# Idle products of TensorE removed at five places of a hybrid decoder layer

## The reference

```python
mix = hybrid_mixer(x, ...)                       # ends in: merged @ w_out
x = layer_norm(ALPHA * x + mix, ln1_g, ln1_b)
aff = sigmoid(x2 @ router_w); sel = aff + router_bias
# best group of experts by its two best sel; the two best experts in it
gate = w_sel / sum(w_sel)
# tokens are sorted by expert into blocks of 128
h = silu(xblk @ w_gate[e]) * (xblk @ w_up[e]);  y = h @ w_down[e]
x = layer_norm(ALPHA * x + sum of the token's two gate * y, ln2_g, ln2_b)
```

## Time and profile before

| | us |
|---|---|
| median of three runs | 2181.05 |
| the profiled execution | 2181.75 |
| its span | 2179.9 |
| attention, 705 to 860 | 155 |
| output projection's last part and choice, 1500 to 1526 | 26 |
| routing, 1526 to 1540 | 14 |
| experts, 1540 to 2129 | 589 |
| joining, 2129 to the end | 51 |

### The profile page before, as it was taken

One profiled execution on the slowest core, in us unless ns is written; L12 is line 12 of the kernel. 1 busy time (PEld: TensorE's weight loads), 2 busy tenths in 40 slices (PEclk: granted clock), 3 DMA queues, 4 the chain that ended last, 5 costly groups with the idle time before them and its releaser, 6 DMA issues. The chain is left out here.

```text
span 2179.9 us, 36484 instructions
## 1 busy us (share of the span) xinstructions
PE 2088.2 (96%) x14738; PEld 1681.1 (77%) x14739; DVE 1267.1 (58%) x1270; ACT 928.4 (43%) x1067; POOL 504.1 (23%) x357
## 2 busy tenths in 40 slices
PE   8999999999999999999999999998799999999996
PEld 6777777766787787888887788787588888888882
DVE  4767322224411465346478713455788888888885
ACT  4662122233101464022245421001577777777763
POOL 3332211113250001333423332200122222222200
PEclk9999999999999999999999999999799999999998
DMA  4445634434430543321143422121799999999986
GB/s 153 134 118 188 182 101 117 113 96 157 171 135 24 137 110 125 137 68 48 48 131 115 168 90 97 61 78 58 295 406 389 383 383 382 382 376 382 380 336 236
DMA packets 138136, 408.48 MB, mean 187 GB/s; under 512 B 38736, under 2 KB 60112, under 8 KB 112800
## 3 DMA queue, kind: packets, MB, share of 16 engines
q1 hardware_dynamic: 122528, 363.21, 48.3%
q10 hardware_dynamic: 6128, 26.22, 3.1%
q0 software_dynamic: 9360, 17.32, 2.1%
HBM read 353.53 MB, written 69.93 MB: 194 GB/s over the span
## 5 line engine op out<-in xcount | busy, mean ns | idle before, releaser
L3458 DVE TENSOR_TENSOR ex_sb_low<-landed,high 128x2048 fp32r<-128x2048 f32 x192 | 431.1, 2287 | 66.1 <-ACT high L3387 63.8
L3387 ACT CAST high<-landed 128x2048 fp32r<-128x2048 f32 x186 | 345.9, 1910 | 40.2 <-PE ex_ps_u L166 37.3
L3272 POOL DMA_INDIRECT y_rows<-ex_sb_y,slot_row x32 | 32.2, 1007 | 443.3 <-ACT ex_sb_y L3402 425.1
L164 PE MATMUL ex_ps_g<-high,ex_sb_xt 128*128 128x512 f32 x260 | 106.0, 408 | 2.4 <-DVE ex_sb_xt L3452 2.4
L164 PE MATMUL ex_ps_u<-high,ex_sb_xt 128*128 128x512 f32 x260 | 102.3, 394 | 0.4 <-DVE ex_sb_low L3458 0.4
L166 PE MATMUL ex_ps_g<-high,ex_sb_xt 128*128 128x512 f32 x260 | 102.5, 394 | 0.0
L165 PE MATMUL ex_ps_g<-ex_sb_low,ex_sb_xt 128*128 128x512 f32 x260 | 102.1, 393 | 0.0
L166 PE MATMUL ex_ps_u<-high,ex_sb_xt 128*128 128x512 f32 x260 | 101.7, 391 | 0.0
L165 PE MATMUL ex_ps_u<-ex_sb_low,ex_sb_xt 128*128 128x512 f32 x260 | 100.9, 388 | 0.0
L164 PE MATMUL ex_ps_y<-high,ex_sb_ht 128*128 128x512 f32 x248 | 97.5, 393 | 0.0
L1113 DVE TENSOR_TENSOR rc_sb_ab<-rc_ps_m,mats 128x512 f32<-128x512 f32 x32 | 20.6, 686 | 132.2 <-PE rc_ps_m L981 132.2
(11 more groups left out here) (663 smaller groups left out, 5567.9 us busy)
## 6 DMA issues: line engine op xcount, KB each, us to landing
landed<-exp_gate SPq DMA_DIRECT2D x62, 1024.0 KB, 7.3
landed<-exp_up SPq DMA_DIRECT2D x62, 1024.0 KB, 8.0
landed<-exp_down SPq DMA_DIRECT2D x62, 1024.0 KB, 8.1
chunk_ch<-slab SPq DMA_DIRECT2D x4, 2048.0 KB, 7.5
merged_d<-room SPq DMA_DIRECT2D x16, 512.0 KB, 2.9
mixer_oT<-ssm_c SPq DMA_DIRECT2D x16, 512.0 KB, 4.8
cb_sb_y<-y_rows SPq DMA_DIRECT2D x16, 512.0 KB, 9.6
si_sb_w<-w_tiles SPq DMA_DIRECT2D x14, 512.0 KB, 3.6
```

Of the source, the lines that this page charges most:

```text
L164: nc.tensor.matmul(out, lhs[0], rhs[0], start=start, stop=False)
L3272: pool.indirect_dma_start(k.y_rows, bass.IndirectOffsetOnAxis(ap=k.slot_row[:, e:e + 1], axis=0), y[e % 2][:, :], None, bounds_check=2 * T ...
L3387: nc.scalar.copy(part_half(high[part], h), part_half(k.landed[part], h)).then_inc(high_ready[part], 1)
L3458: nc.vector.tensor_tensor(part_half(low[part], half), part_half(k.landed[part], half), part_half(high[part], half), ALU.subtract).then_inc ...
```

## The change

All five groups of idle products are removed (54 products, 58 matrix instructions, as the routing's four are two instructions each), with the names that held their counts and the PSUM tile `ps_idle`. In the output projection the wait in front of them goes too (`mixed`, NT + 1); `turn`, which comes next, waits for `x1_ready`, which VectorE signals later. Nothing else is moved.

```diff
@@ fox_attend
                               (k.x_high, k.x_low)).then_inc(gate_done, 1)
-                keep_streaming(nc, k, ps_short[:, :], 12)
                 mm = nc.tensor.matmul
@@ out_project
                 logits(NT - 2, 0)
-                pe.wait_ge(mixed, NT + 1)
-                for n in range(IDLE_PRODUCTS):
-                    mm(ps[0][:, n % 2, :], high[1][:, n % KD, :], w_high[n % 4][:, 0, 0:HALF], start=True, stop=True)
                 turn(NT - 1, 1)
@@ route
                 mm(ps_rank[:, :, :], mat(k, "ones"), by_tile[2], start=False, stop=True).then_inc(ranked, 1)
-                for n in range(IDLE_PRODUCTS):
-                    mm(ps_idle[:, :], mat(k, "ident"), k.mats[:, 0:HALF], start=True, stop=True)
                 for j in range(2):
@@ experts
-                for n in range(IDLE_AT_HEAD):
-                    nc.tensor.matmul(ps_y[:, n % 2, :], high[0][:, 0:P], high[0][:, 0:HALF], start=True, stop=True)
                 turn_x(0, 0)
@@ combine
-                for n in range(IDLE_PRODUCTS):
-                    nc.tensor.matmul(ps[1][:, 1, :], k.high[n % 3][:, 0:P], k.high[n % 3][:, 0:HALF], start=True, stop=True)
                 for t in range(NT):
```

More of the change, by code:

```diff
@@ L166, in times @@
     return nc.tensor.matmul(out, lhs[1], rhs[0], start=False, stop=stop)
-def keep_streaming(nc, k, out, n):
-    for i in range(n):
-        nc.tensor.matmul(out, k.x_high[:, i % KD, 0:P], k.x_high[:, i % KD, 0:HALF], start=True, stop=True)
 def project_parts(nc, out, w, x, halves=(0, 1)):
@@ L2832, in out_project @@
         rows = [s.sb(n, [P, NT * EG]) for n in ("best", "first", "second", "g_one", "g_best")]
-        picks, IDLE_PRODUCTS = s.sem("picks"), 18
+        picks = s.sem("picks")
         ps = [s.ps(f"t{b}", [P, 2, HALF]) for b in range(2)]
@@ L3087, in route @@
         ps_rank, ps_count, ps_slots = s.ps("rank", [P, NT, E]), s.ps("count", [P, HALF]), s.ps("slots", [P, HALF])
-        ps_idle, IDLE_PRODUCTS = s.ps("idle", [P, HALF]), 4
         (last, picked, counted, ranked, listed, slots_done, high_done, done, cleared, set_again, tokens_ready) = (s.sem(n) for n in (
@@ L3218, in experts @@
         ended, block_expert, over_row = s.sb("ended", [P, 16, E]), s.sb("block_expert", [P, 16]), s.sb("over_row", [P, 16])
-        IDLE_AT_HEAD = 8
         used = [s.sem(f"used{i}") for i in range(3)]
@@ L3726, in combine @@
         out_rows = k.out.rearrange("a (n p) d -> (a n) p d", p=P)
-        IDLE_PRODUCTS = 12
         with s.block() as block:
```

## The result

The change makes the kernel slower by 0.22%: the ratio of after to before is 1.0022, with a 95% interval of 1.0013 to 1.0031. The medians of 15 executions each are 2188.27 us (after) and 2182.39 us (before); the ratio stands for 4.8 us, 2.8 to 6.8. (It is not the quotient of these two medians, which lie 5.9 us apart.) The prediction was 2185.9 us, 4.1 us more than the profiled execution of before. The median of after lies within its range, 2183.0 to 2189.3, and 2.4 us above the forecast; 0.6 of these come from the base, since the fifteen executions of before have a median that much above the profiled one (2181.75), on which the sum was made.

A forecast was written before the change was run, and what follows sets the result against it. TensorE, busy for 96% of the span, was taken to bound the kernel. Attention 0, output projection +2.5, routing -0.5, head 0 and joining +2.1 gave +4.1 on the profiled 2181.75: 2185.9 us, range 2183.0 to 2189.3.

The forecast's parts named there:

- Output projection, +2.5: Last tile: without the 18 products, transposes (+0.9) and narrow products (+1.6) run at the low clock; bounds +0.9 and +2.9 us.
- the first reason: Output projection: TensorE would stop for 4.4 us, longer than the stop that cost the clock at 718.6.
- The second reason: Output projection: products ahead of the stop are narrow ones, behind which the clock fell also at 1520.7.
- Joining, +2.1: Joining stage: first tile starts at the low clock, losing 2.4 us, 0.31 given back; bounds +1.7 and +3.1 us.
- Routing, -0.5: Routing: listing products end 0.7 us earlier without idle ones ahead, most of it kept through the gather; bounds 0 and -1.6.
- the bound 0: Routing: no gain if the first expert's weights set when the gathered rows land.
- Attention, 0: Attention: nothing stands behind the twelve products and the clock fell in spite of them, so scores start low either way; 0 us.
- the first rival: Attention pays too, where the clock usually survived the 2.8 us stop: up to 3 us more, 2188.9 us; chance 0.17.
- Head, 0: Head of the experts: transposes and gate products already ran at the low clock, so removing eight products changes nothing.
- The second: Rival: only one of output projection and joining stage pays in full; about 2184 us; chance 0.16.
- The third: Rival: faster, as idle products delay the routing's listing products; gain 0.7 to 1.6 us, 2180.2 to 2181.0; chance 0.05.
- The fourth: Rival: every microsecond at the low clock costs a half, busy or not; +9.1 us, 2190.9 us; chance 0.04.

The follow-up runs named there:

- the best version: Kernel before, with the first expert's last weights third loaded later, 24 idle products in the attention, six at the head, eight behind the first transposes: ratio 0.9979, median 2178.17 us.

## Why the prediction was right, point by point

**Output projection, +2.5: right in its size.** The clock was lost ahead of `turn`, though not for the first reason that I gave: I argued from the length of the stop, 4.4 us against 2.8, and the clock fell 1.4 us into it. The second reason, that the products ahead of the stop are narrow ones, fits better with what the other kernels show (last section). The narrow products do slow down like the transposes: `turn` +0.88 (forecast +0.9), `logits` +1.66 (+1.6), 2.55 at the start of the routing. The one choice in it, the transposes' ratio of 1.8 carried over to 32-column products, holds: 3.63 / 1.97 = 1.84. The removal alone shows 2.54 in the stage and +2.4 us in the time. In executions that lose the clock during `logits` even with the 18 products, the step from `turn` to the routing takes 10.1 to 10.6 us in place of 9.8, and the removal costs that much less.

**Joining, +2.1: right.** The first join is 2.62 us later and 2.35 of it arrive at the end; 0.27 are given back, about the 0.31 us wait that was named, which is gone in after. The clock came back 5.3 us after the first product, past the 4.9 that gave the middle and under the 6.3 of the upper bound. The removal alone gives 2.19 to the end.

**Routing, -0.5: the wrong term.** The step to the listing is right against the profile that it was made from (0.78 us earlier, forecast 0.7), which had one of the late listings; against the mean of ten it would be 0.2. What failed above all is the step behind it: I carried most of the gain through the gather, and the bound 0, the weights set when the rows land, was the true value. In after the rows are even 0.39 us later against the routing's start, and with the routing's products alone removed they are level. The weights' part in it is shown: take the last third of the weights out of the way, and the rows come 2.3 us earlier with or without the listing's gain.

**Attention, 0, and the first rival: the clock is lost with the twelve products and without.** The removal alone leaves the stage where it was, and no profile with twelve products kept the clock. The step "so the scores start at the low clock too" did not hold in after: TensorE stood for 3.93 us ahead of the first score, longer than in any profile with the products, and the scores still began at the full clock and lost it 1.4 us later. So the length of the stop alone does not tell when the clock falls, neither here nor ahead of `turn`, and the 0 came out partly by luck. The first rival (2188.9 us) comes nearest to the median of after, 2188.27, yet its mechanism is not what happened: the stage of after is not longer. The distance from the forecast's 4.1 us to the measured 4.8 is within the interval, and with the routing at nothing the forecast would have been 4.6. The interval is 4 us wide, so the time alone bears out little; the stages do.

**Head, 0: right.** The eight products can be left out, and the cover is VectorE's wait: the 0.9 us that bridging to the full clock gives is taken back there in its profile. The slice with the low clock, where the routing and the head lie, is the 29th of the page and not the 31st.

**The other rivals.** The second (about 2184, only one place pays) falls, since both places paid in full in their stages. The third (faster, the listing's products in the way) had its mechanism, the earlier listing, but not its gain. The fourth priced every microsecond at the low clock at a half, which is the rule of the Trainium skill, TensorE: Matmul & The Clock Gate, section Terms; it gave +9.1 us, and the interval of 2.8 to 6.8 excludes it. The low clock cost only what TensorE ran in it with someone waiting: from 1511 to 1514 of after it was idle at 0.50 and lost nothing. The same is seen in before, in a stretch that the prediction names and the earlier trace rows does not have:

```profile
1522.00:1528.00 6.00, 0.00 (x0) 0.00 (x0) 4.51 (x19) 0.00 (x0) 1.15 (x3) 0.50 0.15 22
```

Of what I named as signs of a wrong prediction, one came true: the gather lands as late as before relative to the weights.

## What to carry to other kernels

Price an idle product by the work behind the stop: here it is worth about half a microsecond for each microsecond of dense or chained TensorE work that would else run at the low clock with someone waiting for it, and nothing where another engine or a transfer ends last. Then look in the granted clock whether it bridges the stop at all: twelve that ended 1.6 to 2.8 us before the data came lost the clock all the same in the attention, and twelve that ended 0.72 us before it kept it in the joining stage. And follow a gain to the next thing that ends late; an early gather issue was worth nothing behind the weights that were queued ahead of it, and moving a third of these gained 2.8 us, about as much as the best set of idle products is worth (2.4).

## What the runs showed of the hardware that I had not expected

- A gather issued by GpSimd moved no packet for 4.1 us while one other queue held the 16 DMA engines at 98 to 103%, and began 1.7 us after its issue where that queue had run down. The Trainium skill, DMA: Bandwidth & Descriptors, section Queues, rings and completion order, says that each engine takes the queues with work in turn, a packet at a time. The traces don't show such sharing until the weights are nearly through; whether the gather's descriptors were ready before that, while the weights moved, no run here shows.
- The 32-column products, a weight load each, slow down with the clock nearly as much as dense ones: 1.84 times, against 1.95 for the joining's products (0.86 / 0.44 us).
- The clock was lost during `logits` itself in four kernels that still had the 18 products: 2.30, 2.66, 2.73 and 2.76 us instead of 1.97 (`logits` in the table). In the best version the granted clock reads 1.00, 0.60 and 0.50 in the three single microseconds of its `logits`, in which TensorE is busy without a gap (stretches, columns as above):

```profile
1520.00:1521.00 1.00, 0.88 (x8) 0.88 (x8) 0.00 (x0) 0.06 (x1) 0.00 (x0) 1.00 0.02 4
1521.00:1522.00 1.00, 1.00 (x8) 1.00 (x7) 0.00 (x0) 0.00 (x0) 0.00 (x0) 0.60 0.00 0
1522.00:1523.00 1.00, 0.78 (x4) 0.64 (x3) 0.00 (x0) 0.19 (x1) 0.00 (x0) 0.50 0.00 0
```
